# Value pages of the paged cache in three slots instead of two, each group asked for one step sooner

## What is computed

```
def page_step(carry, p):
    phys = page_table[:, p]
    kp = cache_k[phys].astype(F32).reshape(DB, PAGE_SIZE, B_HEADS, 2, B_DH)
    vp = cache_v[phys].astype(F32)
    s = jnp.einsum('bthcd,bkhcd->bhctk', qs, kp) + alibi(p * PAGE_SIZE + jnp.arange(PAGE_SIZE))
    return merge(carry, s, vp), None        # running softmax, acc += pe @ vp
```

```
mix = o.astype(x.dtype).reshape(B, T, B_WIDTH) @ b_w_o[j]
```

## Time and profile before

| | |
|---|---|
| median of 3 runs | 1545.45 us |
| lowest and highest run | 1541.03 and 1554.92 us |
| the profiled execution's own time | 1551.45 us |
| its span, first to last instruction | 1549.4 us |
| its mean granted TensorE clock | 0.926 |
| TensorE matmul busy | 1330.6 us (86%) |
| VectorE busy | 747.6 us (48%) |
| ScalarE busy | 397.8 us (26%) |
| mean DMA rate over the span | 224 GB/s |

### The profile page before, as it was taken

One profiled execution on the slowest core, in us unless ns is written; L12 is line 12 of the kernel. 1 busy time (PEld: TensorE's weight loads), 2 busy tenths in 40 slices (PEclk: granted clock), 3 DMA queues, 4 the chain that ended last, 5 costly groups with the idle time before them and its releaser, 6 DMA issues. The chain is left out here.

```text
span 1549.4 us, 28645 instructions
## 1 busy us (share of the span) xinstructions
PE 1330.6 (86%) x11207; PEld 765.5 (49%) x11207; DVE 747.6 (48%) x1930; ACT 397.8 (26%) x1076; POOL 168.3 (11%) x242
## 2 busy tenths in 40 slices
PE   6999989988799998867999997777878699999890
PEld 3445555555555755533445643444444255755550
DVE  3344666666565321117015643778876465421116
ACT  3023444443211121114000311344344411121112
POOL 1012332232101000011000001000000001000002
PEclk9999999998899799988999999889898899799995
DMA  6142334123532899952108889999998941899925
GB/s 221 55 143 80 105 107 132 60 70 105 187 135 85 336 367 354 330 200 91 52 28 290 343 309 387 375 393 380 396 359 310 315 204 62 302 375 348 328 75 180
DMA packets 132155, 347.55 MB, mean 224 GB/s; under 512 B 22012, under 2 KB 51887, under 8 KB 123824
## 3 DMA queue, kind: packets, MB, share of 16 engines
q1 hardware_dynamic: 116036, 315.47, 56.3%
q0 software_dynamic: 4992, 17.83, 3.1%
q10 hardware_dynamic: 10988, 12.36, 2.5%
HBM read 302.09 MB, written 43.52 MB: 223 GB/s over the span
## 5 line engine op out<-in xcount | busy, mean ns | idle before, releaser
L397 PE MATMUL bank<-wring,xT 128*128 128x512 f32 x512 | 232.8, 610 | 1.3 <-DVE attn_q_xT L378 1.3
L397 PEld LDWEIGHTS bank<-wring,xT 128*128 128x128 f32 x512 | 97.5, 195 | 119.7 <-issue 117.9
L836 PE MATMUL bank<-xT,wring 128*128 128x512 f32 x256 | 115.8, 609 | 10.2 <-DVE hgrn_g L671 10.2
L1378 PE MATMUL bank<-wring,xT 128*128 128x512 f32 x256 | 120.2, 623 | 2.0 <-DVE xT L1298 2.0
L2506 DVE STREAM_TRANSPOSE attn_q_xT<-attn_q_xT 128x1024 f32<-128x1024 f32 x64 | 76.5, 1221 | 43.2 <-DMA attn_q_xT<-cache_k 43.2
L2506 DVE STREAM_TRANSPOSE wring<-wring 128x1024 f32<-128x1024 f32 x64 | 76.3, 1224 | 26.1 <-DMA wring<-cache_k 25.8
L836 PEld LDWEIGHTS bank<-xT,wring 128*128 128x128 f32 x256 | 49.1, 195 | 73.4 <-issue 59.9
L1378 PEld LDWEIGHTS bank<-wring,xT 128*128 128x128 f32 x256 | 49.8, 201 | 60.1 <-issue 59.9
L745 DVE COPY_PREDICATED gla_att<-level_masks,bank 128x512 f32<-128x512 int32 x48 | 35.1, 731 | 60.8 <-PE bank L856 60.7
L2044 PE MATMUL bank<-attn_q_xT,wring 128*128 128x512 f32 x128 | 55.5, 593 | 0.0
L856 PE MATMUL bank<-gla_qe,gla_ke 128*128 128x128 f32 x384 | 50.8, 289 | 0.4 <-DVE gla_att L745 0.3
(11 more groups left out here) (429 smaller groups left out, 2317.3 us busy)
## 6 DMA issues: line engine op xcount, KB each, us to landing
wring<-cache_k SPq DMA_DIRECT2D x64, 512.0 KB, 6.3
attn_q_xT<-cache_k SPq DMA_DIRECT2D x64, 512.0 KB, 7.4
wring<-cache_v SPq DMA_DIRECT2D x56, 512.0 KB, 6.7
xT<-cache_v SPq DMA_DIRECT2D x48, 512.0 KB, 7.4
moe_wd<-moe_w_down SPq DMA_DIRECT2D x20, 1024.0 KB, 13.6
wring<-moe_w_gate SPq DMA_DIRECT2D x18, 1024.0 KB, 12.2
wring<-moe_w_up SPq DMA_DIRECT2D x18, 1024.0 KB, 15.9
wring<-a_w_in SPq DMA_DIRECT2D x16, 1024.0 KB, 10.2
```

What stands on the lines that cost most here:

```text
L397: last = nc.tensor.matmul(bank[:, :], xT[:, c, cols(t)], w[:, c, :], start=(c == 0), stop=(c == DC - 1))
L836: last = nc.tensor.matmul(bank[:, :], lhsT, k.xT[:, c, 0:SEQ], start=(c == 0), stop=(c == DC - 1))
L1378: last = nc.tensor.matmul(bank[:, :], k.xT[:, c, cols(t)], w[:, c, :], start=(c == 0), stop=(c == DC - 1))
```

## The change

Values from V5 on go round three places, 0, 1 and 5. SyncE's slot s asks for V(s-5) after waiting for value(s-8); before, it asked for V(s-6) after waiting for the same value(s-8). Slot 12 asks for V7 as well. At the end V28 is in place 5, V29 and V30 in the key slots, V31 in place 1 as before, and the halves of `b_w_o` are asked for after fewer finished value groups: the first when 27 are done (28 before) and ahead of V31, the second when 29 are done (31 before). V31 waits for 28 (27 before). The core of the diff:

```
-VALUE_SLOT = [2] * V_EARLY + [(s - V_EARLY) % 2 for s in range(V_EARLY, STEPS - 4)] + [3, 4, 5, 1]
+VALUE_SLOT = [2] * V_EARLY + [(0, 1, 5)[(s - V_EARLY) % 3] for s in range(V_EARLY, STEPS - 3)] + [3, 4, 1]
...
                         values_in(V_EARLY + 1)
                         new_values(sp, 1)
+                        values_in(V_EARLY + 2)
                         sp.wait_ge(proj.v_out, len(V_UNITS))
                         proj.store(sp, v, "v_prompt", None, proj.v_stored)
-                    v_s = s - LAG
-                    if v_s >= V_EARLY + 2:
-                        sp.wait_ge(valued, v_s - 1)
+                    v_s = s - LAG + 1
+                    if v_s >= V_EARLY + 3:
+                        sp.wait_ge(valued, v_s - 2)
                         values_in(v_s)
                         if v_s % GROUPS_ == 1:
                             new_values(sp, v_s // GROUPS_)
                 sp.wait_ge(valued, STEPS - 6)
-                values_in(STEPS - 5)
+                values_in(STEPS - 4)
                 for s in range(2):
                     sp.wait_ge(scored, STEPS - 1 + s)
-                    values_in(STEPS - 4 + s)
-                values_in(STEPS - 2)
+                    values_in(STEPS - 3 + s)
                 sp.wait_ge(valued, STEPS - 5)
+                k.load_weights(sp, column_halves(a["b_w_o"][0], 0))
+                sp.wait_ge(valued, STEPS - 4)
                 values_in(STEPS - 1)
                 new_values(sp, DEC_B - 1)
-                sp.wait_ge(valued, STEPS - 4)
-                k.load_weights(sp, column_halves(a["b_w_o"][0], 0))
-                sp.wait_ge(valued, STEPS - 1)
+                sp.wait_ge(valued, STEPS - 3)
                 k.load_weights(sp, column_halves(a["b_w_o"][0], HB))
```

## The result

| | before | changed |
|---|---|---|
| median | 1548.6 us (4 runs, 1541.03 to 1554.92) | 1571.87 us (4 runs, 1570.82 to 1573.64) |
| ratio | | 1.0165, 95% interval 1.0129 to 1.0202 |
| span of the profiled execution | 1549.4 us | 1569.5 us |
| from K12's issue to the next stage's first transfer | 1229.01 - 940.31 = 288.7 us | 1248.58 - 936.99 = 311.6 us |

The change made the kernel 23.3 us slower, where 5.1 us had been forecast. All of it lies between K12 and the end of the stage: in the two profiled executions, whose spans differ by 20.1 us, this part is 311.6 - 288.7 = 22.9 us longer.

The account below looks back on a forecast made before the run. The prediction took the stage to be bound by a loop of key loads, transposes and scores, with values riding along with slack. Its terms, 0 + 5.1 + 0 = 5.1 us, on 1545.45 gave 1550.6 us, range 1541 to 1560.

Parts of the forecast that it names:

- What bounds the stage: Stage from K12 on: a loop of keys, transposes and scores sets the pace; value matmuls wait for no transfer.
- Steady state "nothing": Slots 13 to 32: same wait count and bytes between key groups, so SyncE's and key waits stay; 0 us.
- The sign I had named for it: In the changed profile, SyncE's total wait for line 2408 still about 40 us.
- V7 ahead of K13, 5.1 us: Slot 12: one more value group in a full queue delays K13 by 5.1 us, between 3.6 and 6.3.
- where I had named 17: Sign in the changed profile: VectorE's idle time before K13's first page near 17 us instead of 11.96.
- The next step of the prediction: After K13: queue and engine chain both move by 5.1 us, and the shift goes through to the stage's end.
- the first rival: Slots after K13: the shift is absorbed in thin stretches with 13.4 us of unused rate; price 0, 1545.5 us; chance 0.21.
- The end: Stage's end, V28 to V31 and halves of `b_w_o`: the new order is covered by 3.5 us of slack; price 0.
- V31's second condition: Stage's end: value(27) done, taken as met at 1200.4, before V31's issue at 1203.88.
- The second, faster by 21.4 us: SyncE passes its waits sooner, so VectorE's key waits beyond K13's, 21.4 us, go; 1529.2 us; chance 0.08.
- The third, slower by more through clock and V31: Longer TensorE idle before score(13) lowers the clock, 2.6 us, and V31 misses slack, 1.6 us; 1554.8 us; chance 0.15.
- The chances of 0.87 for no change and 0.07 for slower: Whole kernel, with one per cent (15.5 us) as the threshold: no change 0.87, slower 0.07, faster 0.06.

Follow-up runs that it names:

- experiment 2: Kernel before, with only the new values of each sequence asked for one slot sooner: 1568.48 us, ratio 1.016.
- experiment 8: Kernel before, with two of the five loads of new values asked for one slot sooner: 1557.17 us, ratio 1.0059.
- experiment 1: Changed kernel, with the new values asked for one slot later, in the slot of the kernel before: 1548.45 us, ratio 1.0009.
- experiment 5: Changed kernel, with the new values asked for behind the next keys instead of ahead of them: 1548.05 us, ratio 1.0012.
- experiment 3: Changed kernel without the lead: three places, each value group in its old slot waiting for value(s-9), new values a slot later than before: 1543.72 us, ratio 1.0.
- experiment 4: Changed kernel with new values in their old slot, V7 in its old slot and V11 right behind V10 instead: 1554.13 us, ratio 1.0029.
- experiment 6: Kernel before, with one extra 2 MiB group that nothing reads put ahead of K13 in slot 12: 1551.69 us, ratio 1.0041.
- experiment 7: Kernel before, with four extra groups that nothing reads, at the end of slots 12, 16, 20 and 24: 1561.62 us, ratio 1.0087.

## Why the prediction was wrong

**What bounds the stage: right.** The value matmuls wait for no transfer in the changed kernel either. Keys do set the pace, and that is why holding them costs.

**Steady state "nothing": the step that failed.** I compared the count of `valued` in both kernels, found it equal, and wrote that "SyncE's waits therefore stay" and that "queued behind them are only the transfers named". Two lines further down in the same slot stands a second wait, `new_valued`, under a condition on v_s. Raising v_s by one moved it, together with its load, one slot sooner against everything else, and I costed it at zero without looking at it: the sum has no term for it. The load is 16 KB, and its size says nothing of its price. The term measured 22.8 us for the five waits alone (experiment 2), that is 4.6 each, and two of them cost two fifths of it (experiment 8). Taking it out brings the kernel back to 1.0009 (experiment 1), and so does keeping the wait and moving only the keys ahead of it, 1.0012 (experiment 5). The sign I had named for it was there too: SyncE's wait for line 2408 should have stayed at about 40 us and was 26.3. The numbers were in the trace before: K15's issue at 980.38 directly after score(13), and line 2415 of the same slot behind it.

The price of one is smaller than the wait, 44.3 us in 5 places being 8.9 each. Of that, 4.6 reach the end. One part of the wait falls in time in which K(s+1) could not yet have been asked for: for K15, SyncE stood 11.7 us, from 976.77 to 988.45, and the first 4.9 of them were before score(13) had ended. Another part comes back in the queue, which had emptied: K15's pages landed 4.8 us after their issue (median), against 8.9 in the kernel before. So VectorE's wait for K15 grew from 2.1 us to 4.9 only.

The clock is a part of what does reach the end. For the same 2357 matmuls between K12 and the stage's end TensorE was busy 231.5 us in the changed kernel and 227.2 in experiment 2; in the other eight profiles it was 213.4 to 224.3, with 224.3 in the kernel before. In each of the five places the placing matmuls show it, at 3.5 to 3.6 us instead of 1.9. How the 4.6 us divide between late data and the clock was not separated.

The Trainium skill, "DMA: Bandwidth & Descriptors", section "Anatomy of one DMA — SWDGE (gpsimd) path", says that DMA engines do not wait on semaphores and that any wait happens on the issuing sequencer before dispatch. The section is about transfers that GpSimd issues. These runs, whose transfers SyncE issues, agree, 8.2 us for K15: the order of waits on an issuing queue is part of each transfer's price behind it.

**V7 ahead of K13, 5.1 us: the term right where it arises; less of it arrives, and where it goes is open.** In the changed kernel VectorE's idle time before K13's first page is

```profile
970.41 1.25 DVE L2506 STREAM_TRANSPOSE attn_q_xT<-attn_q_xT 128x1024 f32<-128x1024 f32 x1 [17.51 <-DMA attn_q_xT<-cache_k]
```

17.51 - 11.96 = 5.6 us more, where I had named 17. The next step of the prediction was that no event is left to hold the shift back. Experiment 1, which has V7 and not the moved wait, seems to contradict it:

```profile
939.61 3.60 SPq L1985 DMA_DIRECT2D wring<-cache_k  x4
...
980.89 3.37 PE L2375 MATMUL bank<-attn_q_xT,sa_q 128*32 128x128 f32 x64 [12.07 <-DVE attn_q_xT L2506]
...
991.86 1.96 PE L2375 MATMUL bank<-wring,sa_q 128*32 128x128 f32 x64
```

score(13) is 41.3 us after K12's issue (35.7 before), score(14) 52.3 (51.1 before), as if 4.4 of 5.6 us were made up between two scores. But experiment 5, which has V7 in the same place, makes up nothing:

```profile
976.03 3.64 PE L2375 MATMUL bank<-attn_q_xT,sa_q 128*32 128x128 f32 x64 [12.63 <-DVE attn_q_xT L2506]
...
991.46 1.95 PE L2375 MATMUL bank<-wring,sa_q 128*32 128x128 f32 x64
```

With its K12 asked for at 934.66 these are 41.4 and 56.8 us. All ten profiles side by side, in us; scores are counted from K12's issue:

| kernel | extra group ahead of K13 | TensorE idle before score(13) | score(13) | score(14) | between |
|---|---|---|---|---|---|
| before | no | 6.43 | 35.7 | 51.1 | 15.4 |
| experiment 2 | no | 7.96 | 35.8 | 51.3 | 15.5 |
| experiment 8 | no | 8.07 | 36.2 | 51.7 | 15.5 |
| experiment 3 | no | 7.58 | 36.1 | 47.4 | 11.3 |
| experiment 4 | no | 6.96 | 36.5 | 48.1 | 11.6 |
| experiment 5 | yes | 12.63 | 41.4 | 56.8 | 15.4 |
| changed | yes | 11.99 | 41.2 | 52.3 | 11.0 |
| experiment 1 | yes | 12.07 | 41.3 | 52.3 | 11.0 |
| experiment 6 | yes | 13.14 | 41.0 | 52.5 | 11.5 |
| experiment 7 | yes | 12.61 | 41.1 | 52.0 | 10.9 |

The group ahead of K13 moves score(13) by 5.2 us (41.2 against 36.0 in the mean). The work between the two scores takes about 11 us or about 15.5, and both occur with and without the group. The difference is TensorE's clock. Right behind score(13), the turning of the weights (line 2387) takes 3.68 us, at the lower level, in the four kernels with 15.4 or 15.5, and 2.0 to 2.4 us in the other six; over 8 us there the granted clock was 0.60 in the kernel before and 0.89 in experiment 1. Compared at the same clock, the shift is still there at score(14): 56.8 against 51.1 to 51.7, and 52.0 to 52.5 against 47.4 to 48.1. Experiments 1 and 3, alike in this clock, are still 4.1 us apart at score(20) (1054.25 - 939.61 = 114.6 and 1048.74 - 938.27 = 110.5).

So the profiles bear out the step as far as they can be compared. The times do not bear it out to the end of the stage: by experiments 1, 6 and 7, of one group that is repaid at the end, 1.4 us stay (-1.2 to 4.0); of one that is not, 6.3 (0.5 to 12); of four, 13.5. That less than 5.1 us arrives rests on the one interval of experiment 1; experiment 5 has the same V7, and its interval (-4.3 to 7.9 us) holds 5.1. The time of experiment 1 is that of the first rival, which I had put at 0.21; where in the stage a shift would be absorbed, no run shows.

**The end: right.** V31's order and the halves of `b_w_o` cost nothing that shows. value(31) followed the units ahead of it with no idle time, and experiment 1, which has the same end, is level with the kernel before. One reading was off: V31's second condition was not met ahead of its place in the list. SyncE asked for V31 at 1221.06, 1.1 us after value(27) had ended at 1218.03 + 1.93; value(31) began 18.9 us after V31's issue, with no idle time, so it cost nothing.

**The rivals.** The second, faster by 21.4 us, fell in the form I gave it; experiment 3 built what it asked for and found 0. The third, slower by more through clock and V31, had the right side for the wrong reason. Its longer idle time came (11.99 us for 6.43), but the clock behind it was no lower in the changed kernel, and V31 cost nothing; the lower clock came elsewhere, behind the held keys. Its 1554.8 us is 17 us short. The chances of 0.87 for no change and 0.07 for slower rested on a list of causes that lacked the one at work.

## What to carry to other kernels

On a queue that issues transfers in order, the wait ahead of a transfer prices everything behind it, whatever the transfer's size; when an index in a list of waits is shifted, recompute every condition that uses it, not only the one meant. For each wait write down the instruction that meets it and compare it with the instruction that meets the wait of the next critical transfer: here score(s-1) stood between value(s-8) and value(s-7), and crossing it once a sequence cost 4.6 us each. More buffers pay only for a reader that waits; the trace said that this one did not.

## What the runs showed of the hardware

A group of transfers put ahead of a critical load in a full queue (407 to 413 GB/s) moved that load by about its own transfer time: 2 MiB ahead of K13 moved score(13) by 5.2 us in the mean of five kernels against five, and 2.097/0.409 is 5.1.

TensorE's clock behind an idle time was not set by the length of that time. After 12.63 us of it the lower level lasted through score(13) and the turning behind it (score to score 15.4 us), after 12.07 us it did not (11.0); after 6.43 us it did (15.4), after 6.96 us it did not (11.6). So a difference of 4 us between two single profiles of this stage can be the clock alone. The same shows in the runs: the six fastest of experiment 3, 1538 to 1541 us, had a mean granted clock of 0.930 to 0.933, and its two slowest, 1557 us, had 0.916 and 0.920.

A stage whose transfers ran at 393 GB/s from 958 to 1180 us (experiment 3) was not faster beyond the scatter than one at 375: there VectorE's waits for keys were nearly the same, 30.8 us against 33.4, and SyncE stood for scores instead of values.
